# Two decoder layers on eight cores: opening in four steps, modulation scheduled apart from the norms, unpadded pool states

## Chip, cores and metric

The kernel runs on all 8 cores of one Trainium2 chip. Each core takes one prompt sequence (2048 tokens) and 16 of the 128 sample sequences (8 tokens each, 128 tokens together); nothing is exchanged between the cores. The metric is the device time of the slowest core in microseconds (us), lower is better.

## What is computed

Two layers over 1024 features. Every sublayer begins with an RMSNorm whose output is scaled and shifted by a modulation of the sequence's conditioning vector, and ends in a gated residual add. The part that the change touches, cut from the reference:

```
mod = silu(c) @ w_ada[l] + b_ada[l]                 # (B, 6D): 48 features of 128 a layer
sh1, sc1, g1, sh2, sc2, g2 = split(mod, 6)
h = rmsnorm(x, norm_mix[l]) * (1 + sc1) + sh1
# layer 0, mixer 0:
proj = h @ w_in0                                    # 1024 -> 2048
a, xin, bg, cg = split(proj, [512, 1024, 1536])
ya  = (trailing means of a over windows 2,4,8,16, minus a) @ w_pool, one 128x128 a group, * s_pool
yc  = depthwise causal conv (width 3) of cg * xin ;  yb = bg * yc
x   = x + g1 * (concat(ya, yb) @ w_out0)
# layer 1: a gating mixer of 128-position chunks instead
# every layer: x = x + g2 * (gelu(ga) * va) @ ffn_down, with ga, va = conv3(h @ ffn_up)
```

The sample sequences carry states in; that of the pooling is the last 15 rows of `a` of each sequence (`state_pool`).

## The kernel before, in words

Everything lies feature-major: 128 features on the partitions, tokens along the free dimension. A core's tokens are two streams: A is the first 1024 prompt tokens and the 128 sample tokens, B the other 1024 prompt tokens, with 8 features of x each in `xa`, `xs_t` and `xb` and the normalised input of a matmul in `ha` and `hb` (bf16). The stages follow in program order: mixer0(A), mixer0(B), ffn(A), ffn(B) and so on; while a stage runs on one stream, the next norm of the other stream is put between its pieces.

A Python program adds operations one after another to five engines' lists (`Sched`, L30): each list runs in that order, waits are derived from what an operation reads and writes. So the code's order is the order on each engine, and an operation that waits holds everything behind it on its engine. Three things set it around the change:

- Weights. Seven slots `wsl0` to `wsl6` hold a 1024x256 piece each (1 MB read as f32, 0.5 MB written as bf16 by a DMA of the POOL queue). `W.tick` (L340) issues the next piece of the list of uses for every slot that has come free; the pieces come in the order in which the program asks for them (`W.get`, L322). One bf16 piece of `w_ada` makes two features of the modulation: `g_ada` (L633) does 16 matmuls 128x17 into the bank `pN` and has DVE add the bias into `mod`; for scale features a second DVE operation follows.
- The background. `bg_stage` (L433) gives a stage a list of generators, and `pump` (L451), which is called between the pieces of a stage, advances them so that they are through after 17 of 20 parts of the calls. Before, norm and modulation are one list, woven one to one by `g_weave` (L583). A norm (`g_norm`, L574) squares the stream on ACT into `hb` or `ha` (scaled by 1/32), sums over the features with matmuls against ones into `pN` (`sums`), takes the power -0.5 on POOL, spreads the result over the partitions by matmuls (`bcast`), and applies it on DVE (`bg` from x, scale and rstd) and ACT (shift into `hb`).
- The opening (`program`, L1299), written by hand: x of A in two halves of 512 tokens (`load_x`), the squares, sums and scaling of each half (`scale_x` writes x times rstd into `xb`, which is free until B is loaded), the first eight modulation pieces between them (0 to 3 give the shifts, 4 to 7 the scales), and then `affine`, 16 operations on ACT and DVE by turns that make `ha`.

mixer0 (L743) runs four pool features P (input features 0 to 3) and four conv units C, of which each takes three features x, c and b. `P_open` (L758) does P0 and P1 of A together, 32 matmuls, k outermost. For the samples a pool feature needs its own extended row, 16 sequences times (15 old + 8 new) in a part of `R` (`ext_of`). Before, the host pads the states to that shape and four DMAs load them there; ACT then writes the 8 new columns of each sequence over the padding, and so waits for the load. `P_S2` (L795) is the pooling on DVE: up to four shifted additions of 1024 columns, the same for the samples, the subtraction. `P_S2b` (L833) is the 128x128 matmul of a group, `C_S1` (L859) a conv unit, `C_end` (L903) its product with b.

```
            act(E[2][:, 0:1024], PP[prx][:, :], AF.Copy, PK(prx), EK(2, 0, 1))
            if i >= 1:
                C_end(i - 1)
            else:
                P_S2(3)
            C_pre(i)
```

Of the kernel before, what the change touches and what calls it, by code (L numbers as in the profile page):

```python
# [152 lines left out]
def build_program():  # L153
# [12 lines left out]
    stp_d = din("stp", [128, 4, 16, 23])  # L166
# [264 lines left out]
    BG = {"early": [], "gens": [], "armed": True, "calls": {}, "subs": {}, "stage": None, "c": 0, "done": 0}  # L431

    def bg_stage(name, early, gens, armed):  # L433
        assert not BG["gens"] and not BG["early"]
        BG.update(stage=name, early=list(early), gens=list(gens), armed=False, c=0, done=0)
        if armed:
            bg_arm()

    def bg_sub():
        while BG["early"] or (BG["armed"] and BG["gens"]):  # L440
            q = BG["early"] or BG["gens"]
            try:
                next(q[0])
                if BG["armed"]:
                    BG["done"] += 1
                return True
            except StopIteration:
                q.pop(0)
        return False

    def pump():  # L451
        W.tick()
        if not BG["armed"]:
            bg_sub()
            return
# [12 lines left out]
    def bg_end():  # L468
# [3 lines left out]
        BG["calls"][BG["stage"]], BG["subs"][BG["stage"]] = BG["c"], BG["done"]  # L472
# [78 lines left out]
    def g_stats(st):  # L551
        nt = 3 if st.samp else 2
        for ti in range(2):
            for k0 in (0, 4):
                sq_main(st, ti, range(k0, k0 + 4))
                yield
# [3 lines left out]
        yield  # L560
        for ti in range(nt):
            sums(st, ti)
# [5 lines left out]
        yield  # L568
        bcast(st)
        yield  # L570
        rcopy(st)
        yield

# [8 lines left out]

    def g_weave(main, side, r):  # L583
        ms, ss, c = list(main), list(side), 0
        while ms or ss:
            q = ss if ss and (not ms or c % (r + 1) == r) else ms
            c += 1
            try:
                next(q[0])
                yield  # L590
            except StopIteration:
                q.pop(0)
# [40 lines left out]
    def g_ada(l, s):  # L633
# [16 lines left out]
        yield  # L650
# [91 lines left out]

    def mixer0(st):  # L743
# [13 lines left out]

        def P_open():  # L758
            sl = slots["a"] = W.get(("in0", 0))
            prs = [newpair(), newpair()]  # L760
            for ti in range(2):
                for k in range(8):
                    for g in range(2):
# [763 lines left out]
```

How the kernel before makes its waits and increments, by code:

```python
            def body(e, ops=ops, eng=eng):  # L134
                for op in ops:
                    for y in op.need:
                        if y.dma:
                            e.wait_ge(lane_sems[(y.eng, y.lane)], 16 * (y.gen + 1))
                        else:
                            e.wait_ge(sems[y.eng], y.val)
                    ins = op.fn(e)
                    if op.dma:
                        ins.then_inc(lane_sems[(eng, op.lane)], 16)
                    elif op.sig:
                        ins.then_inc(sems[eng], 1)
```

## Time and profile before

| what | value |
|---|---|
| median of 3 runs | 1557.12 us (1555.64 to 1557.77) |
| profiled execution, its own time | 1556.27 us |
| span of the profiled core (7, the slowest) | 1554.6 us |
| spans of the 8 cores | 1548.3 to 1554.6 us |
| PE / DVE / ACT / POOL busy | 92% / 67% / 51% / 21% of the span |
| chain of waits, share by engine | PE 79%, DVE 6%, ACT 6%, issue 4%, DMA 4% |
| mean granted TensorE clock | 0.979 |

The profile is that of the slowest core: of 1554.6 us its TensorE (PE) is busy for 1436.9. The other figures are read in that light: where PE is busy all the time, another engine's work costs nothing, and the 118 us in which it is not are what a new order of the work can win. The page's slices show where they lie: in forty slices PE is at 9 tenths or more from the fifth to the thirty-ninth, and at 1, 6, 5 and 8 tenths in the first four.

### The profile page before, as it was taken

The page shows a single profiled execution, that of the slowest core. Times are in us where ns is not written, and L with a number is a line of the kernel's source. Part 1 is how long each engine was busy: PE and PEld are TensorE (multiplying, and loading weights), DVE is VectorE, ACT ScalarE, POOL GpSimd, SP SyncE. Part 2 cuts the span into 40 slices and gives each one's busy share as a digit, 9 for nine tenths or more (in the row PEclk, how much of TensorE's full clock was granted, in tenths as well). Part 3 has the DMA queues.
Part 4 walks back from the last instruction along what each step waited for, and adds up shares of the span by engine and source line. Part 5 has one row for each costly group of instructions (what it writes and reads, how often), then busy time and mean ns, then how long its engine had stood idle before and what let it go on. Part 6 is the DMA issues. An engine that isn't in the chain of part 4 may idle for free.

```text
span 1554.6 us, 26494 instructions; the slowest of 8 cores (1548.3 to 1554.6 us)
## 1 busy us (share of the span) xinstructions
PE 1436.9 (92%) x9294; PEld 752.6 (48%) x9294; DVE 1037.4 (67%) x1071; ACT 793.2 (51%) x966; POOL 326.6 (21%) x769
## 2 busy tenths in 40 slices
PE   1658999999999999999999999999999999999996
PEld 1334544445545544444456566544554444444444
DVE  1656557568687777759754533656768977677886
ACT  2235145457475555737555425445746654664552
POOL 2112112112232122223212101112212222222210
PEclk9979999999999999999999999999999999999998
DMA  9957656654568645445643821644444454446523
GB/s 209 201 133 126 96 83 102 114 95 77 105 111 132 121 69 94 83 82 90 118 71 63 150 42 28 101 79 83 88 80 80 74 87 68 81 76 138 124 45 109
DMA packets 62678, 151.93 MB, mean 98 GB/s; under 512 B 13010, under 2 KB 28498, under 8 KB 62036
## 3 DMA queue, kind: packets, MB, share of 16 engines
q0 software_dynamic: 33984, 120.34, 48.4%
q1 hardware_dynamic: 28564, 29.90, 6.2%
q8 instruction: 76, 1.25, 0.3%
q14 instruction: 54, 0.44, 0.1%
HBM read 252.68 MB, written 17.85 MB: 174 GB/s over the span
## 4 chain that ended last, share of the span: by engine, by line
PE 79%; DVE 6%; ACT 6%; issue 4%; DMA 4%; POOL 1%; DVEq 0%; ACTq 0%; POOLq 0%; SPq 0%
PE pp L382 72%; PE pS L382 5%; PE pN L382 2%; DMA wsl<-w_ada 2%; DMA xb<-xp 1%; ACT hb L401 1%; ACT E L401 1%; ACT Y L401 1%; DVE Y L404 1%; ACT ha L401 1%; DVE Y L408 1%; DVE ha L404 1%; DVE bg L404 1%; DVE xb L408 1%; DVE xb L404 1%
## 5 line engine op out<-in xcount | busy, mean ns | idle before, releaser
L404 DVE SCALAR_TENSOR_TENSOR Y<-E,par_t,Y 128x1184 f32<-128x1184 f32 (+1 forms) x368 | 502.2, 1367 | 246.1 <-ACT Y L401 232.3
L382 PE MATMUL pp<-ha,wsl 128*128 128x512 bf16 (+1 forms) x1840 | 427.6, 384 | 6.8 <-DVE ha L1328 3.8
L382 PE MATMUL pp<-R,wsl 128*128 128x512 bf16 (+2 forms) x1928 | 421.8, 375 | 0.8 <-DVE xb L404 0.4
L382 PE MATMUL pp<-hb,wsl 128*128 128x512 bf16 x1792 | 399.9, 382 | 3.7 <-DVE xb L404 2.9
L401 ACT ACTIVATE E<-pp 128x1024 f32<-128x1024 f32 x192 | 196.1, 1022 | 329.6 <-PE pp L382 325.4
L382 PEld LDWEIGHTS pp<-R,wsl 128*128 128x128 bf16 x1928 | 185.2, 98 | 212.0 <-issue 1.7
L382 PEld LDWEIGHTS pp<-hb,wsl 128*128 128x128 bf16 x1792 | 174.9, 98 | 214.0 <-issue 11.5
L401 ACT ACTIVATE Y<-E,par_t 128x1184 f32<-128x1184 f32 (+1 forms) x184 | 240.6, 1307 | 67.0 <-DVE R L408 17.2
L382 PEld LDWEIGHTS pp<-ha,wsl 128*128 128x128 bf16 x1840 | 176.9, 99 | 201.1 <-issue 21.1
L411 POOL COPY cffn<-E 128x2 f32<-128x2 f32 x176 | 78.2, 444 | 442.5 <-ACT E L401 442.5
L408 DVE TENSOR_TENSOR R<-Y 128x1184 bf16<-128x1184 f32 (+1 forms) x86 | 112.2, 1305 | 5.8 <-ACT Y L401 5.4
L401 ACT ACTIVATE Y<-Y 128x1184 f32<-128x1184 f32 (+1 forms) x88 | 97.7, 1110 | 17.3 <-DVE Y L404 17.2
L404 DVE SCALAR_TENSOR_TENSOR xa<-pp,mod,xa 128x1024 f32<-128x1024 f32 x64 | 79.9, 1279 | 33.8 <-PE pp L382 33.8
L404 DVE SCALAR_TENSOR_TENSOR xb<-pp,mod,xb 128x1024 f32<-128x1024 f32 (+3 forms) x80 | 83.5, 1066 | 27.1 <-PE pp L382 27.1
L401 ACT ACTIVATE Y<-pp 128x1024 f32<-128x1024 f32 x33 | 33.5, 1016 | 114.8 <-PE pp L382 78.3
L370 POOL DMA_DIRECT2D wsl<-ffn_up x88 | 46.8, 532 | 189.1 <-PE pS L382 86.6
L382 PE MATMUL pN<-sc_t,wsl 128*128 128x17 bf16 x768 | 26.8, 172 | 61.3 <-DMA wsl<-w_ada 31.4
L382 PE MATMUL pS<-ha,wsl 128*128 128x128 bf16 x896 | 69.2, 221 | 10.5 <-ACT E L401 6.2
L382 PEld LDWEIGHTS pS<-ha,wsl 128*128 128x128 bf16 x896 | 57.7, 99 | 35.0 <-issue 18.9
L401 ACT ACTIVATE E<-pS 128x128 f32<-128x128 f32 x92 | 24.4, 265 | 89.0 <-PE pS L382 82.9
L401 ACT ACTIVATE hb<-xb 128x512 bf16<-128x512 f32 (+2 forms) x88 | 46.0, 580 | 35.2 <-DVE xb L404 23.9
L382 PEld LDWEIGHTS pN<-sc_t,wsl 128*128 128x128 bf16 x768 | 25.4, 98 | 73.3 <-issue 66.9
(110 smaller groups left out, 1011.6 us busy)
## 6 DMA issues: line engine op xcount, KB each, us to landing
wsl<-ffn_up POOLq DMA_DIRECT2D x88, 512.0 KB, 5.6
wsl<-w_ada POOLq DMA_DIRECT2D x48, 512.0 KB, 8.2
wsl<-ffn_down POOLq DMA_DIRECT2D x32, 448.0 KB, 4.9
wsl<-w_in POOLq DMA_DIRECT2D x16, 512.0 KB, 8.0
wsl<-w_out POOLq DMA_DIRECT2D x16, 512.0 KB, 6.9
wsl<-ffn_down POOLq DMA_DIRECT2D x16, 512.0 KB, 5.4
wsl<-w_uv POOLq DMA_DIRECT2D x16, 512.0 KB, 6.9
o_ffn_s<-E SPq DMA_DIRECT2D x88, 80.0 KB, 4.9
```

The lines of the kernel that those rows point to most:

```text
L370: add("pool", lambda e, s=s, src=src, n=n: e.dma_start(out=wsl[s][:, 0:n], in_=src), writes=[("w", s)], dma=True)
L382: add("pe", lambda e, l=l, r=r, i=i: e.matmul(out_ap, lhsT=l, rhs=r, start=(start and i == 0), stop=(stop and i == n - 1)), reads=rk, writ ...
L401: add("act", lambda e: e.activation(out=out, in_=in_, func=func, **kw), reads=reads, writes=writes)
L404: add("dve", lambda e: e.scalar_tensor_tensor(out=out, in0=in0, scalar=scalar, in1=in1, op0=op0, op1=op1), reads=reads, writes=writes)
L408: add(eng, lambda e: e.tensor_tensor(out=out, in0=in0, in1=in1, op=op), reads=reads, writes=writes)
L411: add("pool", lambda e: e.tensor_copy(out=out, in_=in_), reads=reads, writes=writes)
```

## The change

Six edits:

1. Opening. The DVE share of the second half's squares goes to ACT; modulation pieces 2 and 3 come later; pieces 4 to 7 are each followed by the affine operations of two features (both halves), and the 32 matmuls of P0 and P1 are done in four groups of eight (`open_k`), each one step behind its affine operations. The weights of P0 and P1 are asked for before modulation piece 4.
2. `W.tick()` stands in `setup` behind the loads of x instead of ahead of it.
3. The background has two lists. Norms are advanced as before; modulation is a `side` list of its own, at most two half pieces a call, spread over 97% of a stage's calls (from a quarter on in mixer0(A)), and no new piece starts between a norm's sums and its rstd copy (`lock`). A norm squares two features a step instead of four. In mixer0(A) the norm of B starts after 16 idle steps (before, 10).
4. In C unit 0 the pooling of group 3 (`P_S2(3)`) moves from behind the x matmuls to behind the c product on DVE, and the first conv operation on ACT to behind the b copy.
5. The pool states come unpadded (128x960) in one DMA to a place of their own; POOL copies them into the extended rows, four copies of 16x15.
6. ACT's writing of the new sample columns no longer waits for the load.

```
@@ pump
-        n, c = BG["subs"][BG["stage"]], BG["calls"][BG["stage"]]
+        (n, m), c = BG["subs"][BG["stage"]], BG["calls"][BG["stage"]]
         target = -(-n * BG["c"] * 20 // max(1, 17 * c))
         while BG["done"] < target:
             if not bg_sub():
                 break
+        f = (BG["c"] / c - BG["s0"]) / (0.97 - BG["s0"])
+        for _ in range(2 if BG["sdone"] + 3 < m * f else 1):
+            if BG["sdone"] < m * f and not (BG["lock"] and BG["sdone"] % 2 == 0):
+                bg_sub("side", "sdone")
@@ g_stats
-            for k0 in (0, 4):
-                sq_main(st, ti, range(k0, k0 + 4))
+            for k0 in range(0, 8, 2):
+                sq_main(st, ti, range(k0, k0 + 2))
                 yield
...
+        BG["lock"] = True
         for ti in range(nt):
             sums(st, ti)
...
+        BG["lock"] = False
@@ mixer0
+        def ext_hist(g):
+            sa, sk = rsp_f32(5120, 960)
+            pcopy(ap3(exts[g][0], 23)[:, :, 0:15], ap3(sa[:, g * 240:(g + 1) * 240], 15), sk, [("exh", g)])
...
                 act(ap3(a, 23)[:, :, 15:23], v3(so[g][0]), AF.Copy, so[g][1], k)
+                ext_hist(g)
@@ C_S1
             if i >= 1:
                 C_end(i - 1)
-            else:
-                P_S2(3)
...
+            if i == 0:
+                P_S2(3)
+            else:
+                yinit()
@@ program
-        adas(0, 2)
+        adas(0, 1)
         sums(A_, 0)
         rstd_pow(0, 4)
-        adas(2, 3)
+        adas(1, 2)
         bcast_part(0)
         scale_x(0)
-        for k in range(8):
-            if k % 2 == 0:
-                sq_main(A_, 1, (k,))
-            else:
-                stt(A_.h[:, k, 512:1024], xseg(A_, k, 512, 512), 1.0 / 1024, xseg(A_, k, 512, 512), ALU.mult, ALU.mult,
-                    xK(A_, k, 1), hK(A_, k, 1))
-        adas(3, 5)
+        sq_main(A_, 1, range(8))
         sums(A_, 2)
         sums(A_, 1)
         rstd_pow(4, 5)
-        adas(5, 6)
+        adas(2, 3)
         bcast_part(1)
         bcast_part(2)
-        adas(6, 7)
+        scale_x(1)
...
-        scale_x(1)
-        adas(7, 8)
-        for ti in range(2):
-            for k in range(8):
-                affine(ti, k, "act" if k % 2 == 0 else "dve")
+        adas(3, 4)
+        open_get()
+        for q in range(4):
+            adas(4 + q, 5 + q)
+            for ti in range(2):
+                for k in (2 * q, 2 * q + 1):
+                    affine(ti, k, "act" if k % 2 == 0 else "dve")
+            if q >= 1:
+                open_k(A_, (2 * q - 2, 2 * q - 1))
...
-        bg_stage("m0A", [], [g_idle(10), g_weave(norm_gens(B_, 0), ada_gens(0, 8, 18), 1)], True)
+        open_k(A_, (6, 7))
+        bg_stage("m0A", [g_idle(16)] + norm_gens(B_, 0), ada_gens(0, 8, 18), True, 0.25)
```

The order on the engines shows three places. First PE in the opening: `sc_t` rows are modulation pieces, `ones_bf` rows the sums, `ident` rows the broadcasts, `pp<-ha` the matmuls of P0 and P1.

```order
-L382 MATMUL pN<-sc_t,wsl 128x17 x32
-L382 MATMUL pp<-ha,wsl 128x512 x32
+L382 MATMUL pN<-sc_t,wsl 128x17 x48
+L382 MATMUL pp<-ha,wsl 128x512 x8
+L382 MATMUL pN<-sc_t,wsl 128x17 x16
+L382 MATMUL pp<-ha,wsl 128x512 x8
+L382 MATMUL pN<-sc_t,wsl 128x17 x16
+L382 MATMUL pp<-ha,wsl 128x512 x16
```

The last two modulation pieces now stand between the groups of the opening's matmuls.

Second, ACT in mixer0(A), behind the copy of P2 out of PSUM (`E<-pp`); `hb<-xb` are the squares of B, `R<-pN,par_t` and `R<-pp,par_t` the copies of a finished pool group, `E<-pS` and `E<-pp` those of a feature. Before:

```order
L401 ACTIVATE E<-pp 128x1024
L401 ACTIVATE hb<-xb 128x512 x4
L401 ACTIVATE R<-pN,par_t 128x16x8
L401 ACTIVATE R<-pp,par_t 128x1024
L401 ACTIVATE hb<-xb 128x512 x4
L401 ACTIVATE R<-pS 128x16x8
L401 ACTIVATE hb<-xb 128x512 x4
L401 ACTIVATE E<-pp 128x1024
```

The same place in the changed kernel:

```order
L401 ACTIVATE E<-pp 128x1024
L401 ACTIVATE R<-pN,par_t 128x16x8
L401 ACTIVATE R<-pp,par_t 128x1024
L401 ACTIVATE R<-pS 128x16x8
L401 ACTIVATE E<-pp 128x1024
L401 ACTIVATE R<-pN,par_t 128x16x8
L401 ACTIVATE R<-pp,par_t 128x1024
L401 ACTIVATE E<-pS 128x128
L401 ACTIVATE hb<-xb 128x512 x2
```

The first squares of B stood ahead of the copies of groups 0 and 1 and of P3; now they stand behind them and behind the sample copy of C unit 0's x.

Third, PE around C unit 0 of the changed kernel, from the matmul of pool group 1 (`Y2`, `wsl3`) on; with slot numbers, which tell the weights apart: `wsl6` holds x, `wsl0` c, `wsl1` b, `wsl5`, `wsl4` and `wsl2` modulation.

```order
L382 MATMUL pp0<-Y2,wsl3 128x512 x2
L382 MATMUL pS<-ha,wsl6 128x128 x8
L382 MATMUL pp1<-ha,wsl6 128x512 x16
L382 MATMUL pN<-sc_t,wsl4 128x17 x16
L382 MATMUL pS<-ha,wsl0 128x128 x8
L382 MATMUL pp2<-ha,wsl0 128x512 x16
L382 MATMUL pS<-ha,wsl1 128x128 x8
```

And POOL, which issues the loads of these slots:

```order
L370 DMA wsl5<-w_ada 128x2048
L370 DMA wsl6<-w_in0 128x2048
L370 DMA wsl0<-w_in0 128x2048
L370 DMA wsl1<-w_in0 128x2048
L411 COPY R<-R 128x16x15 x2
L370 DMA wsl4<-w_ada 128x2048
```

The modulation piece in `wsl4` is used between x and c; its load stands behind those of x, c and b and behind two of the new copies, which wait for the states.

## Rows read from the trace of the kernel before

**Rows 1.** Busy time by stretch (us, then busy us and count by engine, clock, DMA)

```profile
0.00:56.60 56.60, 13.14 (x220) 10.98 (x221) 16.40 (x37) 13.00 (x22) 12.30 (x43) 1.00 0.98 194
56.60:156.00 99.40, 73.23 (x587) 38.82 (x588) 58.27 (x92) 43.90 (x70) 14.98 (x34) 0.86 0.76 152
156.00:264.00 108.00, 101.37 (x670) 50.84 (x669) 65.53 (x76) 41.29 (x55) 19.34 (x36) 0.97 0.65 96
```

**Rows 2.** Waits, 66 to 110 us: in total, times, longest

```profile
PE pN L382 <- ACT R L401: 10.6, 1, 10.6
...
PE pN L382 <- DVE mod L408: 5.2, 1, 5.2
...
PE pS L382 <- ACT R L401: 3.4, 1, 3.4
```

**Rows 3.** Timeline, 0 to 70 us: start, busy, what, count

```profile
33.39 2.18 ACT L401 ACTIVATE ha<-xa 128x512 bf16<-128x512 f32 x4
...
42.19 1.41 PE L382 MATMUL pN<-ones_bf,ha 128*128 128x1 bf16 x40 [0.45 <-DVE mod L408]
...
47.99 0.27 ACT L401 ACTIVATE rstd<-pN 128x128 f32<-128x128 f32 x1
...
50.71 4.90 DVE L408 TENSOR_TENSOR xb<-xa,rstd 128x512 f32<-128x512 f32 x8
...
56.61 8.42 PE L382 MATMUL pp<-ha,wsl 128*128 128x512 bf16 x30 [3.77 <-DVE ha L1328]
```

**Rows 4.** DMA issues by window (at 2.9 and 22.9 us): KB, us to landing

```profile
xa<-xp SPq DMA_DIRECT2D x1, 2048.0 KB, 29.4
...
wsl<-w_in POOLq DMA_DIRECT2D x1, 512.0 KB, 28.7
```

**Rows 5.** Timeline, 66 to 170 us

```profile
82.10 2.19 ACT L401 ACTIVATE hb<-xb 128x512 bf16<-128x512 f32 x4 [5.89 <-DMA xb<-xp]
...
98.88 1.01 PE L382 MATMUL pS<-ha,wsl 128*128 128x128 bf16 x8
...
99.69 6.06 PE L382 MATMUL pp<-ha,wsl 128*128 128x512 bf16 x16
...
105.59 0.61 PE L382 MATMUL pS<-ha,wsl 128*128 128x128 bf16 x8
...
112.99 3.62 PE L382 MATMUL pp<-ha,wsl 128*128 128x512 bf16 x16
...
163.74 10.52 PE L382 MATMUL pp<-hb,wsl 128*128 128x512 bf16 x48
```

**Rows 6.** DMA issues by window (at 56.1, 58.4 and 76.0 us): KB, us to landing

```profile
R<-stp SPq DMA_DIRECT2D x1, 184.0 KB, 9.0
...
R<-stp SPq DMA_DIRECT2D x1, 184.0 KB, 13.5
...
wsl<-w_ada POOLq DMA_DIRECT2D x1, 512.0 KB, 15.8
```

**Rows 7.** DMA queues, 65 to 71.5 us, then 71.5 to 82 us: packets, MB, share

```profile
q1 hardware_dynamic: 587, 1.29, 62.0%
q0 software_dynamic: 104, 0.35, 35.7%
...
q1 hardware_dynamic: 162, 2.39, 65.8%
q0 software_dynamic: 150, 0.55, 33.8%
```

**Rows 8.** DVE alone, by stretch: the pooling of groups 1 and 3

```profile
69.60:75.20 5.60, 5.09 (x9) 0.70 0.95 285
99.30:108.45 9.15, 8.32 (x14) 0.71 0.01 2
```

**Rows 9.** POOL, groups by form: busy, mean ns of one

```profile
L411 POOL COPY E<-cpool 128x15 f32<-128x15 f32 x4 | 2.6, 657 | 0.2 <-POOL csc L411 0.2
```

**Rows 10.** Waits of PE, 156 to 264 us

```profile
PE pN L382 <- DVE mod L408: 2.4, 2, 2.1
```

**Rows 11.** Waits of PE, 264 to 500 us

```profile
PE pS L382 <- ACT E L401: 5.1, 4, 2.8
```

More of the change, by code:

```diff
@@ L429, in store, with bg_stage, bg_sub @@
         add("sp", lambda e: e.dma_start(out=out, in_=in_), reads=reads, writes=[("out", octr[0])], dma=True)
[L431 to L441, printed above, removed]
-            try:
-                next(q[0])
-                if BG["armed"]:
-                    BG["done"] += 1
+    BG = {"gens": [], "side": [], "armed": True, "calls": {}, "subs": {}, "stage": None, "c": 0, "done": 0,
+          "sdone": 0, "lock": False, "s0": 0.0}
+    def bg_stage(name, gens, side, armed, s0=0.0):
+        assert not BG["gens"] and not BG["side"]
+        BG.update(stage=name, gens=list(gens), side=list(side), armed=armed, c=0, done=0, sdone=0, s0=s0)
+    def bg_sub(which="gens", cnt="done"):
+        while BG[which]:
+            try:
+                next(BG[which][0])
+                BG[cnt] += 1
                 return True
             except StopIteration:
-                q.pop(0)
+                BG[which].pop(0)
         return False
@@ L471, in bg_end @@
             pass
-        BG["calls"][BG["stage"]], BG["subs"][BG["stage"]] = BG["c"], BG["done"]
+        while bg_sub("side", "sdone"):
+            pass
+        BG["calls"][BG["stage"]], BG["subs"][BG["stage"]] = BG["c"], (BG["done"], BG["sdone"])
     def run(gen):
@@ L568, in g_stats @@
         yield
+        yield
         bcast(st)
@@ L581, in norm_gens @@
         return [g_norm(st, which)]
[L583 to L592, printed above, removed]
     def g_idle(n):
@@ L741, in ext_of, with open_get, open_k @@
         return R_t[:, b // 2: b // 2 + 736].bitcast(F32), RK(b, 1472)
+    opn = {}
+    def open_get():
+        opn["sl"] = W.get(("in0", 0))
+        opn["prs"] = [newpair(), newpair()]
+    def open_k(st, ks):
+        sl, prs = opn["sl"], opn["prs"]
+        for ti in range(2):
+            for k in ks:
+                for g in range(2):
+                    gemm(PP[prs[g]][:, ti * 512:(ti + 1) * 512], PK(prs[g], ti),
+                         [(wap(sl, k, g), st.h[:, k, ti * 512:(ti + 1) * 512])], [("w", sl)], [hK(st, k, ti)],
+                         start=(k == 0), stop=(k == 7))
     def mixer0(st):
@@ L812, in P_S2 @@
                 e3 = ap3(a, 23)
+                k = list(k) + [("exh", g)]
                 c3, lns, ck = e3, 23, k
@@ L885, in C_S1, with yinit @@
             tt(E[ei][:, 2:1026], PP[prc][:, :], E[2][:, 0:1024], ALU.mult, PK(prc) + EK(2, 0, 1), EK(ei, 1))
-            act(Y[ei][:, 0:n], E[ei][:, 2:2 + n], AF.Identity, EK(ei) + ["par"], YK(ei), scale=par(wb + 2),
-                bias=par(P_SCB + i))
+            def yinit():
+                act(Y[ei][:, 0:n], E[ei][:, 2:2 + n], AF.Identity, EK(ei) + ["par"], YK(ei), scale=par(wb + 2),
+                    bias=par(P_SCB + i))
+            if i == 0:
+                P_S2(3)
+            else:
+                yinit()
             pump()
@@ L1286, in setup @@
         load_x(A_, 1)
+        W.tick()
         for g in range(2):
@@ L1376, in program @@
            bgk01 + [("mod", k) for k in range(8)], [("h", 0, k, 2) for k in range(8)])
-        for g in range(4):
-            a, k = ext_of(g)
-            load(a.rearrange("p (b w) -> p b w", w=23), stp_d[:, g, :, :], k, [("mod", 15)])
+        sa, sk = rsp_f32(5120, 960)
+        load(sa, stp_d[:, :], sk, [("mod", 15)])
         load(hist_t[:, :, :, :], sts_d[:, :, :].rearrange("p (r c) w -> p r c w", c=2), [("hist", 0), ("hist", 1)],
```

37 lines of the change are left out of this document (16 added, 21 removed).

## Prediction

> **What bounds the kernel now.** I first read the busy time by stretch, to see where PE is not busy, then the waits of those stretches, then the timeline around each wait for what held the engine that was waited for. Over the whole kernel PE is busy for all but 118 us of its span. Of these, 43.5 us lie ahead of 56.6 us (busy 13.1), 26.2 us in mixer0(A), from 56.6 to 156 us (busy 73.2 of 99.4), and 6.6 us in mixer0(B) [rows 1]. The other 1290 us hold 41 us. So the change can win something in the first two stretches, and little elsewhere.
>
> In mixer0(A) three waits make 19.2 of the 26.2 us: 10.6 for ACT's copies of a pool group, 5.2 for DVE's bias add and 3.4 for ACT's copies of sample columns [rows 2]. The first two have one cause. ACT is in order, and its squares of B stand ahead of the copies (second order excerpt); the squares waited for the load of `xb`, which came at 82.1 us [rows 5]. DVE's add of a modulation piece stands behind ACT's copy through the bank `pN`. So PE stood still until B had landed, twice, once for each half. When it went on, it was slow: 16 matmuls of 512 columns took 6.06 us, against 3.62 for the same 16 at 113 us [rows 5], which is 2.4 us more. The granted clock in the stretch of pool group 3's pooling, which covers them, is 0.71 [rows 8]; half is the lower of the two levels, 1.2 GHz against 2.4.
>
> **Opening.** Each edit on the chain that leads to the 32 matmuls of P0 and P1:
> - The second half of x lands at 2.9 + 29.4 = 32.4 us [rows 4]. Four squares take 2.18 us on ACT [rows 3], so eight take 4.4 and the sums can begin at 36.9 us. Before they began at 42.2, since DVE's share of the squares waited for its scaling of the first half. From the sums' start to the last rstd copy's end 6.1 us pass (42.2 to 48.3), here to 43.0; the half that the scaling needs is copied 0.5 us sooner, 42.5.
> - Scaling takes DVE 4.9 us [rows 3], to 47.4 (before 55.6). From there to the first of the 30 matmuls 1.0 us passed. Now there also lie the sample's scaling, 1.2 (one of the eight scalings takes 0.61, this has twice the columns), and one more modulation piece, about 1.0 (both estimates): first matmul at 50.6.
> - The last modulation piece is bound by its weights. Nine 1 MB pieces come through the POOL queue whatever their order; the ninth, before that of P0 and P1, landed at 22.9 + 28.7 = 51.6 us [rows 4]. Now the ninth is modulation piece 7, and 51.6 stays. It is needed behind two groups of matmuls, after 54 us, so it is not late.
> - The matmuls took 8.4 us [rows 3]. With two pieces between them (0.6 each) and half a microsecond for the alternation with the affine operations, 10.1: the end comes at 61 us, against 65.0. **Minus 4.** Ends: nothing slow and no gap gives 5.5; all 32 at 0.38 us (6.06 / 16 [rows 5]) is 12.1 + 1.2 and gives 1.
>
> `W.tick` behind the loads changes nothing that the chip sees: x goes through SP's list, weights through POOL's, and the first seven loads stay first in POOL's. I cost it at zero; no cover is needed, since it adds no instruction.
>
> **Mixer0(A) up to C unit 0.** The load of the states is issued after the last scale feature, near 58 us. Four padded loads landed 9.0 us (first) to 13.5 us (last) after their issue [rows 6]; the one load with longer rows is nearest to the first: 67 us. ACT no longer waits for it (3.4 us less for PE [rows 2], of which 1.5 stay for ACT's two copies of P0 and P1 at 1.0 each). But POOL copies now wait, and DVE's sample pooling behind them. The nearest row for a copy of 240 columns is POOL's 128x15 copy at 0.66 us [rows 9]; a copy of sixteen times the columns may take no longer, or, at three times that, 2 us. With 0.7 the first is done at 67.7. DVE then has the rest of group 0, 2.3 us (an estimate: one 1024-column operation of 1.2 and small ones), and 5.6 of group 1 [rows 8], done at 75.6. PE needs this for the group 1 matmul that stands ahead of C unit 0 (third excerpt), so x of unit 0 starts at 76 us. Before it started at 98.9 [rows 5]: 23 us ahead. B's squares wait now where nothing of groups 0, 1 and P3 stands behind them.
>
> **The wait that takes its place.** Behind x stands a modulation piece with `wsl4`. Its load is issued only when P0 and P1 have released the slot and POOL has done two copies, at 68 us, and it is fourth in POOL's queue, behind x, c and b. From 61 us SP's two 2 MB loads of `xb` compete. A weight load issued at 76 us amid them took 15.8 us [rows 6]; that would be 84. From 71.5 to 82 us the queues moved 162 and 150 packets, one to one, though SP's carried four times the bytes [rows 7], so a weight piece (about 140 packets) passes for each half of `xb`. Half 1 of `xb` began at 71.5 and took 10.5 us, to 82.1; now they begin near 66, with b beside the first and this piece beside the second: 66 + 2 x 10 = 86. I take 86, near the 84. x is done at 80, so PE stands for 6 us and runs slow behind it, 2.8 us with the sample matmuls.
>
> The Trainium skill (DMA: Bandwidth & Descriptors, Queues, rings and completion order) says that each DMA engine takes its queues by turns, a packet at a time. By it the piece lands with the second half of `xb`, as above, 86. The trace has a stretch that speaks against it: from 65 to 71.5 us SP's queue moved 587 packets to POOL's 104 [rows 7]. At that ratio the piece would land behind both halves, after 91, and the total below would be 5 us higher.
>
> **From c of unit 0 to mixer0(B).** Before, 105.6 to 163.7 us, 58.1 us [rows 5]. Of these 26.2 - 19.2 = 7.0 are PE waits, which I remove; added are the 64 sum matmuls of B, which stood ahead (40 took 1.41 [rows 3], so 2.3), and the slow stretch of 2.8. New waits: DVE now does the c product first and group 3's pooling (9.15 us [rows 8]) behind it, then the taps (3 us) and the unit's product (1.5). With c at 94 us that ends near 109, and c of unit 1 is done near 108; bounded by nothing below and by one pooling, 9 us, above, I take 1.5. 58.1 - 7.0 + 2.3 + 2.8 + 1.5 = 57.7, from 86.5 to 144.2. Before 163.7: **minus 19.5**, the opening's 4 included. The eight later modulation pieces of this stage are the same in number. Their loads find SP's queue empty (the first three are issued near 111, needed from 118), so I cost them at nothing; were `xb` still in flight, one would cost its 15.8 - 7 us.
>
> **Mixer0(B) and later.** In mixer0(B) the sums waited 2.1 us for a modulation add [rows 10] that stood behind group 3's pooling on DVE, and the clock fell: another 2.4 as above. With the pooling behind the c product the add is not held. I take **minus 4**, between 0 (another wait comes) and 6.6, all the idle time there [rows 1]. In ffn(A) PE waits 5.1 us for ACT's copies [rows 11] while four squares at a time stand ahead; two at a time should shorten it: **minus 1**, between 0 and 5.1. The 30 modulation pieces of the later stages are only spaced otherwise.
>
> **Sum.** 19.5 + 4 + 1 = 24.5. The profiled execution took 1556.3 us as a whole (its span is 1554.6), the median of the runs is 0.8 above it: 1556.3 - 24.5 + 0.8 = 1532.6, say **1532 us**.
>
> **Rivals.**
> - *The piece in `wsl4` is in time* (1524 us). If its load gets through beside `xb` as fast as 15.8 us less the queue ahead, near 80, the 6 us wait and the 2.8 of slow clock go: 8.8 less. For it: the row's queue was as full. Against: the packets one to one. Chance 0.17.
> - *The mixer stays late* (1542). The ratio 587 to 104 puts c of unit 0 at 91.5 (5 more), and DVE, which has its pooling behind the c product, passes on some 5 us to unit 1. Chance 0.25.
> - *The four steps don't do what they say* (1536). DVE's and ACT's affine operations and PE wait for each other by turns at the lower clock, and the opening ends where it did, 65: the 4 us are missing. For it: the first matmuls come after 50 us of little work. Chance 0.10.
> - *Slower than before* (1563). The later 30 modulation pieces are no longer woven into the norm's steps. In mixer0(B) one such piece held PE for 2.1 us and cost 2.4 more in clock, 4.5. If that befell the pieces of ffn(A), ffn(B) and mixer1(A), the 24.5 us are gone from the sixth one on; with seven more than the one removed the time is 1532 + 7 x 4.5 = 1563. Against: in the stretch from 264 to 500 us, which holds most of the twelve pieces of ffn(A), no wait for a modulation add is among PE's waits, and ACT's copies are all that it waits for [rows 11]. Chance 0.04.
>
> **Numbers.** The forecast has 0.44, the rivals 0.17, 0.25, 0.10 and 0.04. Its own ends: the opening 1 to 5.5, mixer0(B) 0 to 6.6, ffn(A) 0 to 5.1, the new DVE wait 0 to 9. The range takes in the early piece with a little of ffn(A)'s wait (1524 - 3) and the late mixer with no gain in mixer0(B) and a shorter one in the opening (1542 + 6): 1521 to 1548. A measurement of this kernel can tell 0.2%, 3 us, from no change. All cases but the last are faster by more; 0.02 is kept for a mixture that ends between: faster 0.94, same 0.02, slower 0.04.
>
> **What the changed profile would show.** ACT's wait for `xb` no longer ahead of PE waits; the first matmul of P0 near 51 us, the last near 61; x of unit 0 near 76; PE waiting for `w_ada` near 80 to 86 (none: the first rival); the first matmul on `hb` near 144. I am wrong if that one comes after 155, if the load of the states lands after 72 us, or if PE's idle time behind 264 us has grown by more than 5.

## The result, and the profile after

The change makes the kernel faster: 1542.87 us, the median of 4 runs (1542.21 to 1543.79), against 1557.12 before in the same comparison; the ratio is 0.9906, 95% interval 0.9893 to 0.9919. That is some 14 us less where 25 were forecast, inside the range of 1521 to 1548 and 11 us above the forecast's own 1532. Runs in which the cores of a die were slowed by a disturbance are left out of every time and ratio, here and below.

The page of the changed kernel: its span, busy times, and of the slices PE and PE's clock.

```profile
span 1540.4 us, 26482 instructions; the slowest of 8 cores (1534.2 to 1540.4 us)
...
PE 1431.2 (93%) x9294; PEld 748.5 (49%) x9294; DVE 1035.8 (67%) x1067; ACT 796.6 (52%) x970; POOL 325.3 (21%) x773
...
PE   2668978999999999999999999999999999999996
...
PEclk9989989999999999999999999999999999999998
```

The profiled execution took 1542.21 us. Two things are to be seen: PE's idle time went from 118 us to 109 only, and the first seven slices, the opening and both streams' first mixer, still hold most of it (78 us up to 264 us). Busy time by stretch (us, then busy us and count of PE, PEld, DVE, ACT and POOL, clock, DMA share, GB/s), the stretches of [rows 1] first:

```profile
0.00:56.60 56.60, 18.22 (x235) 13.29 (x236) 16.07 (x35) 16.77 (x28) 11.73 (x42) 1.00 0.99 196
56.60:156.00 99.40, 75.26 (x626) 41.09 (x624) 60.51 (x93) 46.37 (x72) 19.60 (x42) 0.91 0.80 156
156.00:264.00 108.00, 92.05 (x608) 45.55 (x607) 62.26 (x72) 37.26 (x51) 17.68 (x34) 0.93 0.57 88
```

and the last part of the program, from the first matmul of ffn(A) on, in the changed kernel:

```profile
271.80:1540.00 1268.20, 1237.92 (x7799) 645.26 (x7797) 894.46 (x866) 692.76 (x817) 276.25 (x656) 0.99 0.51 91
```

and before:

```profile
268.70:1554.00 1285.30, 1244.45 (x7799) 649.81 (x7797) 894.70 (x866) 692.28 (x817) 279.97 (x656) 0.99 0.51 90
```

With PE's own landmarks as the borders, the 14.2 us of span come about like this, with the wrong sign in the middle row:

| stretch | before | after | difference | forecast |
|---|---|---|---|---|
| start to the first matmul on `hb` | 163.7 | 155.1 | -8.7 | -19.5 |
| mixer0(B), to the first matmul of ffn(A) | 105.0 | 116.7 | +11.7 | -4 |
| ffn(A) to the end | 1285.9 | 1268.6 | -17.3 | -1 |

These are marks of one core, the slowest. Among the eight cores of one execution they differ by 3 to 4 us (the first matmul on `hb` comes at 159.7 to 163.7 before and at 152.9 to 156.2 after), so 2 or 3 us in one cell say little. The medians of the eight cores tell the same here: -8.4, +11.7 and -18.4.

PE's waits from 56 to 156 us: in total, times, longest.

```profile
PE pN L382 <- DVE mod L408: 15.8, 3, 10.7
PE pN L382 <- DVE Y L408: 4.9, 1, 4.9
PE pN L382 <- DMA wsl<-w_ada: 1.9, 1, 1.9
```

The 10.6 us for ACT behind the squares of B [rows 2] are gone. A wait of the same length stands in their place: 10.7 us for DVE's add of a modulation piece. And from 156 to 264 us:

```profile
PE pN L382 <- DVE mod L408: 11.8, 3, 6.5
PE pp L382 <- POOL rs L408: 2.2, 1, 2.2
```

where before DVE's adds made 2.4 us, 2.1 the longest [rows 10]. Both long ones have one picture. DVE's timeline from 90 to 106 us (start, busy, what, count, idle before it and releaser):

```profile
90.91 1.23 DVE L408 TENSOR_TENSOR E<-pp,E 128x1024 f32<-128x1024 f32 x1 [4.33 <-PE pp L382]
92.05 1.23 DVE L408 TENSOR_TENSOR Y<-E 128x1038 f32<-128x1038 f32 x1
93.38 3.90 DVE L408 TENSOR_TENSOR Y<-Y 128x1036 f32<-128x1036 f32 x3
97.20 2.05 DVE L408 TENSOR_TENSOR R<-R 128x352 f32<-128x352 f32 x4
...
102.45 3.02 DVE L404 SCALAR_TENSOR_TENSOR Y<-E,par_t,Y 128x1184 f32<-128x1184 f32 x2 [1.30 <-ACT Y L401]
105.39 0.19 DVE L408 TENSOR_TENSOR mod<-pN,par_t 128x34 f32<-128x34 f32 x1
```

and PE's at its end:

```profile
84.59 0.55 PE L382 MATMUL pN<-sc_t,wsl 128*128 128x17 bf16 x16 [2.04 <-DVE mod L408]
85.00 0.94 PE L382 MATMUL pS<-ha,wsl 128*128 128x128 bf16 x8
...
105.72 0.27 PE L382 MATMUL pN<-Y,wsl 128*128 128x128 bf16 x1 [10.68 <-DVE mod L408]
```

The c product (90.91) is followed by the pooling of group 3 (92.05 to 101.1) and the taps (102.45 to 105.4); the add of the modulation piece that PE has put into `pN` stands behind all of them, and the pool matmul of group 2 needs the same bank. In mixer0(B) it is the sums that need it: 6.48 us at 218.58, with the pooling from 211.76 to 218.3 on DVE.

### The profile page after: what moved, and what is told of

It is laid out like the page before. It is cut to its first block, busy times and chain, and to the rows that moved or that the text cites. A ratio compares the mean times of both kernels' runs of the same rounds, so it can differ in the third digit from the quotient of the medians.

```text
span 1540.4 us, 26482 instructions; the slowest of 8 cores (1534.2 to 1540.4 us)
## 1 busy us (share of the span) xinstructions
PE 1431.2 (93%) x9294; PEld 748.5 (49%) x9294; DVE 1035.8 (67%) x1067; ACT 796.6 (52%) x970; POOL 325.3 (21%) x773
## 4 chain that ended last, share of the span: by engine, by line
PE 80%; DVE 7%; ACT 5%; issue 4%; DMA 3%; POOL 0%; DVEq 0%; SPq 0%; ACTq 0%; POOLq 0%
PE pp L382 73%; PE pS L382 5%; DVE Y L404 2%; DMA xa<-xp 2%; PE pN L382 2%; ACT ha L401 2%; ACT Y L401 2%; ACT E L401 1%; DVE Y L408 1%; DVE R L408 1%; DVE bg L404 1%; DMA R<-stp 1%; ACT hb L401 1%; DVE ha L404 1%; DVE xb L404 1%
## 5 line engine op out<-in xcount | busy, mean ns | idle before, releaser
L382 PEld LDWEIGHTS pS<-ha,wsl 128*128 128x128 bf16 x896 | 57.8, 99 | 30.7 <-issue 15.1
L401 ACT ACTIVATE ha<-xa 128x512 bf16<-128x512 f32 x80 | 43.3, 615 | 17.5 <-DMA xa<-xp 17.5
## 6 DMA issues: line engine op xcount, KB each, us to landing
wsl<-w_in POOLq DMA_DIRECT2D x16, 512.0 KB, 10.1
```

Of the source, the lines that this page charges most:

```text
L382: add("pe", lambda e, l=l, r=r, i=i: e.matmul(out_ap, lhsT=l, rhs=r, start=(start and i == 0), stop=(stop and i == n - 1)), reads=rk, writ ...
L401: add("act", lambda e: e.activation(out=out, in_=in_, func=func, **kw), reads=reads, writes=writes)
```

## Experiments

Each kernel is given by what it changes; `...` marks what is cut from a diff. `hb` is the time of the first matmul on `hb`, then the length of mixer0(B) and of all behind it, from the profile of its slowest core; the last column has the medians of the same three over the eight cores of that execution. The ratio is to the kernel before on the same chip.

| kernel | ratio, 95% interval | hb | mixer0(B) | behind it | medians of 8 cores |
|---|---|---|---|---|---|
| before | 1 | 163.7 | 105.0 | 1285.9 | 162.5, 103.0, 1286.3 |
| changed | 0.9906 (0.9893 to 0.9919) | 155.1 | 116.7 | 1268.6 | 154.1, 114.7, 1267.9 |
| hold | 0.9950 (0.9930 to 0.9969) | 157.2 | 116.8 | 1269.3 | 154.8, 116.2, 1267.8 |
| p3_back | 0.9815 (0.9793 to 0.9838) | 146.5 | 108.0 | 1270.8 | 147.0, 103.8, 1269.7 |
| p3_A | 0.9883 (0.9867 to 0.9899) | 148.6 | 115.0 | 1270.7 | 147.5, 112.3, 1266.8 |
| ps2_only | 0.9883 (0.9868 to 0.9899) | 156.2 | 107.8 | 1270.7 | 154.9, 107.8, 1267.8 |
| e4_only | 1.0054 (1.0036 to 1.0072) | 165.4 | 107.7 | 1288.6 | 164.1, 106.8, 1286.2 |
| no_side | 1.0032 (1.0020 to 1.0045) | 164.7 | 107.4 | 1286.3 | 163.6, 106.0, 1285.1 |
| open_only | 1.0031 (1.0003 to 1.0059) | 168.7 | 111.5 | 1291.7 | 163.8, 107.0, 1292.0 |
| pb_sq4 | 0.9916 (0.9886 to 0.9946) | 157.3 | 104.9 | 1275.2 | 154.9, 105.5, 1273.9 |
| pb_noopen | 0.9862 (0.9842 to 0.9882) | 154.5 | 106.7 | 1271.3 | 151.7, 107.0, 1268.1 |
| pb_padded | 0.9831 (0.9803 to 0.9860) | 149.5 | 109.1 | 1266.8 | 149.7, 105.2, 1267.3 |
| pb_early | 0.9800 (0.9772 to 0.9829) | 144.4 | 108.0 | 1271.0 | 144.7, 104.2, 1267.9 |
| pe_s35 | 0.9857 (0.9836 to 0.9878) | 150.9 | 112.7 | 1267.6 | 149.2, 110.2, 1267.7 |

The profile of open_only is not to be compared stretch by stretch: that execution took 1573.6 us where the median of its runs is 1558.1, and on its slowest core the granted clock was 0.81 from 160 to 230 us although PE was busy all the time.

### Edit 4: the place of the pooling

**p3_back**, the changed kernel with edit 4 undone:

```diff
             if i >= 1:
                 C_end(i - 1)
+            else:
+                P_S2(3)
             C_pre(i)
...
-            if i == 0:
-                P_S2(3)
-            else:
-                yinit()
+            yinit()
             pump()
...
-            if i == 0:
-                yinit()
             for tap in (1, 0):
```

> The changed kernel with its fourth edit undone: the pooling of group 3 behind the x matmuls of unit 0 again, for both streams. Theory: PE's waits of 10.7 us (mixer0(A)) and 6.5 us (mixer0(B)) for a modulation add come from the add standing behind that pooling on DVE while the bank pN is held; with the pooling a product earlier the one in A is at most 3 us, the c product comes 3 us later, and the slow clock behind it goes: 1532 to 1537 us. Rival: DVE is simply short of time there, the wait moves to the c product and to the matmuls behind it: 1542 us, the same.

It took 1526.8 us, a ratio of 0.9815 against 0.9906: edit 4 cost about 15 us (15.1 in the spans). That is 5 us less time than the theory had, and its rival (1542) is out. Both stretches answer, -8.6 up to `hb` and -8.7 in mixer0(B); by the medians -7.1 and -10.9. PE's waits from 56 to 264 us are now many and short, none over 4.1 us:

```profile
PE pN L382 <- DVE mod L408: 13.2, 7, 2.9
PE pN L382 <- DVE Y L408: 4.1, 1, 4.1
PE pS L382 <- DVE mod L408: 3.2, 1, 3.2
```

**hold** asks whether it is the held bank alone: no new modulation piece starts between the issue of the pooling and the pool matmul of group 2 of the changed kernel.

```diff
             if i == 0:
+                BG["hold"] = True
                 P_S2(3)
...
                 P_S2b(n - 2)
+                if n == 4:
+                    BG["hold"] = False
...
-            if BG["sdone"] < m * f and not (BG["lock"] and BG["sdone"] % 2 == 0):
+            if BG["sdone"] < m * f and not ((BG["lock"] or BG["hold"]) and BG["sdone"] % 2 == 0):
```

> The changed kernel, but no new modulation piece begins between the issue of group 3's pooling and the pool matmul of group 2, in both streams; the pooling stays where the change put it. Theory: no matmul result lies in pN while DVE pools, so PE's waits of 10.7 and 6.5 us for the add go, with the 2 to 4 us of slow clock behind each; what stays is DVE's own lateness with unit 1's product, about 5 us: 1526 to 1533 us. Rival: the wait is DVE's load and not the held bank; the same wait stands at the next thing that PE needs from DVE: 1540 us or more.

The pool matmul ran at 92.97 without a wait, and the kernel was still no faster than the changed one: 1548.0, a ratio of 0.9950 against 0.9906. The next rows of PE, and ACT's behind them, show the wait again, on another engine:

```profile
92.97 0.22 PE L382 MATMUL pN<-Y,wsl 128*128 128x128 bf16 x1
93.03 0.59 PE L382 MATMUL pp<-Y,wsl 128*128 128x512 bf16 x2
103.31 0.58 PE L382 MATMUL pN<-sc_t,wsl 128*128 128x17 bf16 x16 [9.69 <-ACT R L401]
```

```profile
99.47 1.37 ACT L401 ACTIVATE Y<-E,par_t 128x1184 f32<-128x1184 f32 x1 [5.15 <-DVE fix L408]
100.75 2.17 ACT L401 ACTIVATE hb<-xb 128x512 bf16<-128x512 f32 x4
102.82 0.35 ACT L401 ACTIVATE R<-pN,par_t 128x128 bf16<-128x128 f32 x1
```

ACT's first conv operation writes a buffer `Y` that the pooling of group 3 still reads, so it waits for the pooling's last operation; squares and the copy out of `pN` stand behind it. The pooling behind the c product thus holds two engines, DVE by its length and ACT through `Y`. In mixer0(B) the hold came too late to keep a piece out, and the sums waited 6.48 us as before. The theory of the bank alone fell; its rival held by the time (1540 us or more), though the next wait was for ACT, which stood behind DVE through `Y`, and not for DVE itself.

**p3_A** undoes edit 4 in stream A alone, **ps2_only** undoes half of it in both streams.

```diff
             if i >= 1:
                 C_end(i - 1)
+            elif st is A_:
+                P_S2(3)
...
-            if i == 0:
+            if i == 0 and st is not A_:
                 P_S2(3)
             else:
                 yinit()
...
-            if i == 0:
+            if i == 0 and st is not A_:
                 yinit()
```

> The changed kernel (1542.87 us) with edit 4 undone in mixer0 of stream A alone. Undone in both streams it took 16 us off (1526.83), of which 8.6 us were there at the first matmul of hb. Theory: the pooling behind the c product costs in each stream by itself, 8 to 9 us in A and the rest in B: 1533 to 1536 us, and the sums of mixer0(B) still wait over 5 us for DVE. Rival: B only inherits what A lost (an earlier A leaves its norm and its loads in time): 1526 to 1529 us.

```diff
             if i >= 1:
                 C_end(i - 1)
+            else:
+                P_S2(3)
...
-            if i == 0:
-                P_S2(3)
-            else:
+            if i != 0:
                 yinit()
```

> The changed kernel (1542.87 us) with only the first half of edit 4 undone: the pooling of group 3 stands behind the x matmuls again, the first conv operation on ACT stays behind the b copy. Theory: the place of the pooling carries the whole cost (it holds DVE's adds of modulation, and ACT through the buffer Y1): 1526 to 1529 us. Rival: the late first conv operation keeps DVE's taps, which stand ahead of the next adds, waiting for ACT by 1 to 2 us a stream and more: 1531 to 1537 us.

Both took 0.9883, some 6 us less than the changed kernel by the spans (1534.2 and 1534.7 against 1540.4), in different places. p3_A has the gain up to `hb` (148.6) and keeps the wait of 6.48 us at the sums: each stream pays by itself, A 6.5 us (155.1 to 148.6; by the medians 6.6) and B 7.0 (115.0 against p3_back's 108.0; by the medians 8.5). Its time, 1536.5, is at the upper end of its theory (1533 to 1536), and the rival that B only inherits is out. ps2_only has nothing up to `hb` (156.2) and its gain in mixer0(B) (107.8, by the medians 6.9 of the 10.9 us that p3_back gains there). So in A the place of the pooling alone is not the matter. DVE of ps2_only after its c product:

```profile
93.13 1.21 DVE L408 TENSOR_TENSOR E<-pp,E 128x1024 f32<-128x1024 f32 x1
101.75 3.02 DVE L404 SCALAR_TENSOR_TENSOR Y<-E,par_t,Y 128x1184 f32<-128x1184 f32 x2 [7.41 <-ACT Y L401]
104.69 0.19 DVE L408 TENSOR_TENSOR mod<-pN,par_t 128x34 f32<-128x34 f32 x1
```

DVE has nothing to do for 7.4 us, because ACT's first conv operation now stands behind the copy of b, which waits for b's matmuls, and the add that PE waits for stands behind the taps. The second half of edit 4 alone (the late conv operation) thus makes the add come at 104.7, as late as both halves together (105.4); the first half alone was not run. In B the add that the sums need is ahead of the taps, and the pooling's place decides most there: the sums start at 213.1 after a wait of 0.2 us. The forecast of 1526 to 1529 for ps2_only failed and its rival (1531 to 1537) held.

**e4_only** is edit 4 alone on the kernel before.

> The kernel before (1556 to 1557 us) with edit 4 alone. Theory: the pooling behind the c product costs by itself, in whatever schedule, since the pool matmul of group 2 shares the bank pN with a modulation piece whose add stands behind it: 1561 to 1572 us, with a wait of PE for DVE of over 5 us between 105 and 125 us. Rival: here the squares of B hold ACT longer and modulation pieces stand elsewhere, so DVE has room for the pooling, and edit 4 is harmful only together with the modulation list: 1554 to 1558 us.

1563.2, slower than before by 8 us, as its theory had it: it costs in the old schedule too. The pool matmul of group 2 waited 4.98 us for the add, and in the kernel before there was no such wait. By the medians 1.6 us of the cost lie up to `hb` and 3.8 in mixer0(B). It is about half of that in the new schedule; a likely reason, not tested, is that PE stood 11.0 us for ACT ahead of it (to 92.9), behind the load of `xb`, which left DVE time.

### The opening

**open_only** is the kernel before with edit 1 (and edit 2, the place of `W.tick`), **pb_noopen** is p3_back with the old opening.

```diff
-        adas(0, 2)
+        adas(0, 1)
...
+        open_get()
+        for q in range(4):
+            adas(4 + q, 5 + q)
...
```

> The kernel before with the opening in four steps and nothing else of the change. Theory: the opening's own gain is real, the last of the 32 first matmuls ends at 60 to 61 us instead of 65, but ACT still waits for the load of B behind it, so PE stands until B has landed as before, and of the 5 us only those 1 to 2 are kept by which B's load is issued earlier: 1555 to 1556 us. Rival: the 5 us pass to the end: 1552 us.

```diff
-        open_get()
-        for q in range(4):
-            adas(4 + q, 5 + q)
...
+        adas(6, 7)
...
+        scale_x(1)
+        adas(7, 8)
...
+        open_get()
+        open_k(A_, range(8))
```

> Base: the changed kernel with edit 4 undone (1526.83 us). Here the opening is that of the kernel before (edit 1 undone). Theory of the prediction (the four steps are worth 4 us, and every us reaches the end because ACT no longer waits for B): the last of the 32 matmuls at 65 us instead of 60.1, and 1530 to 1532 us. Rival: the states, which land at 68.3 us whatever the opening does, take the gain on DVE: 1526 to 1528 us with PE's wait for Y below 1 us.

Alone the four steps bring nothing: 1.0031, the median run 1558.1 us, slower than its theory (1555 to 1556) and far from its rival (1552). Its profile shows PE waiting 6.2 and 9.1 us for ACT's copies between 56 and 100 us; ACT stands in front of the first for the padded states and in front of the second for `xb`. Where ACT waits for neither any more the steps are worth 7.3 us by the spans, 0.9862 against 0.9815; that is more than the 4 us of the theory (1530 to 1532 us against 1534 measured). The opening's own gain is there in both, by its last matmul: 65.0 to 61.4 us in open_only (59.7 on its fastest core), 65.4 to 59.5 from pb_noopen to p3_back. It reaches the end only once nothing behind it waits for a load that comes when it comes. The rival of pb_noopen, that the states' landing takes the gain, did not hold.

### The modulation list and the squares

**no_side** is the changed kernel with edit 3 undone (woven list, ten idle steps, squares by four, and also three idle steps fewer inside a norm and one more in a modulation piece, which belong to the edit), **pb_sq4** is p3_back with squares by four alone.

```diff
-        bg_stage("m0A", [g_idle(16)] + norm_gens(B_, 0), ada_gens(0, 8, 18), True, 0.25)
+        bg_stage("m0A", [g_idle(10), g_weave(norm_gens(B_, 0), ada_gens(0, 8, 18), 1)], [], True)
...
```

> The changed kernel with its third edit undone: norm and modulation woven into one list again, ten idle steps, squares by four. Theory: the squares of B stand ahead of the copies of groups 0 and 1 again, the waits for B of 16 us return, and the later stages (ffn(A), mixer1) lose the some 14 us that they gained: 1557 to 1562 us. Rival: the later gain is not from the third edit; then about 1550 us.

```diff
-            for k0 in range(0, 8, 2):
-                sq_main(st, ti, range(k0, k0 + 2))
+            for k0 in (0, 4):
+                sq_main(st, ti, range(k0, k0 + 4))
```

> Base: the changed kernel with edit 4 undone (1526.83 us). Here a norm squares four features a step instead of two; the side list and its lock stay. Theory: the squares in pairs are what took away PE's waits for ACT in ffn(A), mixer1 and ffn(B) (5.1 us for E from 264 to 500 us, 3.7 for rstd, 3.4 and 4.1 in mixer1 before), so these come back, and 1532 to 1538 us. Rival: the modulation's own list is what took them away (the norm comes through at an even pace), and the size of the steps is worth nothing: 1526 to 1529 us.

Without edit 3 the kernel is slower than the one before (1560.1, as its theory had it), PE waits 10.2 us for ACT behind the load of B again, and the part behind ffn(A) is back at 1286.3 us: all of the 17 us won there are edit 3's. PE's longest wait from 500 to 787 us in no_side is that of before,

```profile
PE pN L382 <- ACT rstd L401: 3.7, 1, 3.7
```

and in the changed kernel none there is longer than 1.8.

pb_sq4 took 1540.9 us, above its theory (1532 to 1538) and its rival (1526 to 1529). Behind ffn(A) it is 4.4 us longer than p3_back (1275.2 against 1270.8), but most of the waits that its theory expected back do not come back: in ffn(A) PE waits 0.7 us for ACT and not the 5.1 of [rows 11], and the 3.7 for `rstd` is absent. What comes is a new single wait of 8.4 us in mixer1(A), where the sums of a norm need the bank of a modulation add:

```profile
827.77 2.96 PE L382 MATMUL pN<-ones_bf,hb 128*128 128x1 bf16 x64 [8.39 <-DVE mod L408]
```

So the late gain does not rest on the squares' size in ffn(A) and ffn(B); at most 4 of the 17 us are the squares' and some 13 the rest of edit 3. Which of the rest does it (the list of its own, its pace, the lock, the idle steps) was not taken apart. In mixer0(A) `hb` comes at 157.3 instead of 146.5 (medians 154.9 and 147.0). PE waits there for an add behind group 3's pooling (4.9), twice for a pooling itself (4.2 together), and 5.2 us for an add that stands behind the taps and the norm's scaling `bg`: no single cause, and which of the shifted pieces costs what stays open.

### The states and the piece in `wsl4`

**pb_padded** is p3_back with the padded states in four loads, **pb_early** is p3_back with the states' load behind modulation feature 5, **pe_s35** is pb_early with the modulation list from 0.35 of the calls on.

```diff
-        sa, sk = rsp_f32(5120, 960)
-        load(sa, stp_d[:, :], sk, [("mod", 15)])
+        for g in range(4):
+            a, k = ext_of(g)
+            load(a.rearrange("p (b w) -> p b w", w=23), stp_d[:, g, :, :], k, [("mod", 15)])
...
```

> Base: the changed kernel with edit 4 undone (1526.83 us). Here the states come padded as in the kernel before, in four loads, so that ACT's writing of the sample columns waits for them and POOL copies nothing (edits 5 and 6 undone). Theory: ACT stands behind the later of the four loads (13.5 us to landing before), the copies of P2 and the pool groups behind it come 2 to 4 us later: 1529 to 1531 us. Rival: DVE needs the states at the same time anyway, and nothing moves: 1526 to 1528 us.

```diff
         adas(3, 4)
+        sa, sk = rsp_f32(5120, 960)
+        load(sa, stp_d[:, :], sk, [("mod", 5)])
         open_get()
...
-        sa, sk = rsp_f32(5120, 960)
-        load(sa, stp_d[:, :], sk, [("mod", 15)])
```

> Base: the changed kernel with edit 4 undone (1526.83 us). Here the load of the pool states is issued behind modulation feature 5 instead of 15, some 10 us earlier. Theory: their landing at 68.3 us sets the start of group 0's pooling on DVE, so PE's wait for Y (4.1 us, 56 to 100 us) goes or falls below 1.5 and x of C unit 0 comes 3 to 5 us earlier: 1521 to 1524 us. Rival: the load shares the queues with the last weights of the opening, whose landing moves by 1 to 2 us, and P0 starts later than 50.5 us by as much; or DVE's own work is the limit: 1526 to 1529 us.

```diff
-        bg_stage("m0A", [g_idle(16)] + norm_gens(B_, 0), ada_gens(0, 8, 18), True, 0.25)
+        bg_stage("m0A", [g_idle(16)] + norm_gens(B_, 0), ada_gens(0, 8, 18), True, 0.35)
```

> The kernel with edit 4 undone and the states' load issued 10 us earlier (1524.1 us, PE standing 7.5 us for the modulation weights in wsl4 between x and c of unit 0), with the modulation list starting at 0.35 of the calls of mixer0(A) instead of 0.25: x, c and b of unit 0 are loaded ahead of the modulation piece, which is used in the middle of c. Theory: the transfer that lands last is in time there, 4 to 8 us go: 1516 to 1520 us. Rival: the queue is full until B has landed, so whatever piece is fourth lands at 84 us, and b or the next modulation piece is waited for instead: 1522 to 1526 us.

pb_padded: 0.9831, from two runs, not to be told from p3_back (0.9793 to 0.9838), so neither its theory nor its rival is settled, although ACT waits there three times for a load (3.90, 2.85 and 4.51 us) and PE 7.5 us for ACT. Edits 5 and 6 move a wait from ACT to DVE and are worth at most a few us.

pb_early: the states are issued at 38.1 us. PE's wait for `Y` went, as forecast, and x of unit 0 begins 5.3 us earlier than in p3_back, at 71.8. c of unit 0 does not:

```profile
71.83 0.61 PE L382 MATMUL pS<-ha,wsl 128*128 128x128 bf16 x8
72.49 3.40 PE L382 MATMUL pp<-ha,wsl 128*128 128x512 bf16 x15
83.41 0.58 PE L382 MATMUL pN<-sc_t,wsl 128*128 128x17 bf16 x16 [7.52 <-DMA wsl<-w_ada]
83.83 1.01 PE L382 MATMUL pS<-ha,wsl 128*128 128x128 bf16 x8
```

The load of this piece was issued at 62.50 and took 20.7 us, to 83.2; in the changed kernel it was issued at 69.07 and took 15.0, to 84.1. Issued 6.6 us sooner it landed 0.9 sooner. With the order changed so that x, c and b come first (pe_s35), c begins at 79.3, but b waits until 88.3 for DVE, which pools group 3, and a modulation piece in mixer0(B) waits 9.3 us for its weights; 0.9857 (1532.6 us, two runs), slower than pb_early. Theory (1516 to 1520) and rival (1522 to 1526) both missed, the rival by less. pb_early, at 1524.1 us and 0.9800, is the fastest of all these kernels and beats the changed one by 1%; the step from p3_back to it is within the intervals.

## Why the prediction was right in its sign and wrong in its size

The forecast said faster by 25 us, and the kernel is faster by 14. It went right up to c of unit 0 and wrong behind it, and the total would be further off but for a gain that it had put at nothing.

- **Opening: right.** First matmul at 50.47 (50.6 forecast), the last of 32 done at 60.15 (61).

```profile
50.47 3.57 PE L382 MATMUL pp<-ha,wsl 128*128 128x512 bf16 x8 [0.69 <-ACT ha L401]
...
56.46 3.69 PE L382 MATMUL pp<-ha,wsl 128*128 128x512 bf16 x16
```

- **Up to C unit 0: right within 2.5 us.** The states were issued at 57.3 and landed 11.0 us later (67 forecast, 68.3 measured), POOL's two copies took 0.72 us together against 0.7 for one. From POOL's row on everything is 1.3 late and DVE's chain another 1.2: x of unit 0 at 78.50 instead of 76.

```profile
68.40 0.72 POOL L411 COPY R<-R 128x240 f32<-128x240 f32 x2 [10.72 <-DMA R<-stp]
...
78.50 0.61 PE L382 MATMUL pS<-ha,wsl 128*128 128x128 bf16 x8
```

- **"The wait that takes its place": the time right, the wait shorter.** The piece landed at 84.1 (86 forecast), and c of unit 0 began at 85.00 (86.5). But x was done only at 82.6 (80 forecast), so PE stood 2.0 us and not 6. The profile puts this to an add behind group 2's pooling, which ended at 84.4; without it the load would have held PE until 84.1, nearly as long. That B's loads set the landing is what pb_early shows. The rival with 587 packets to 104 would have c at 91.5, and is out; so is the one with the piece in time.
- **"From c of unit 0 to mixer0(B)": here it failed.** 57.7 us were forecast, 70.1 came (85.0 to 155.1). PE is idle for 15.7 of them (10.7, 3.1 and 1.9) where the forecast had 1.5, and its busy part, 54.4, is 1.8 below the 56.2 of the sum. Two terms are wrong. "I take 1.5" for the pooling behind the c product, between nothing and 9: it compares the pooling's end with c of unit 1 as a chain of products, and doesn't follow the add that stands behind the pooling in DVE's list, nor ACT behind its conv operation. The wait was 10.7 us, above the bound; what it cost was inside it, since edit 4 undone in A gives back 6.5 (p3_A) to 8.6 (p3_back). And "7.0 are PE waits, which I remove" gives no reason why none should come in their place. With edit 4 undone PE still waits 8.3 us behind c, all for adds of modulation pieces: 3.2 behind group 3's pooling, 1.5 behind the taps, 0.8 and 2.7 behind the norm's scaling `bg`, where the list of its own now puts them. The last of them in p3_back:

```profile
134.48 0.55 PE L382 MATMUL pN<-sc_t,wsl 128*128 128x17 bf16 x16 [2.74 <-DVE mod L408]
...
130.17 4.06 DVE L404 SCALAR_TENSOR_TENSOR bg<-xb,mod,rstd 128x512 f32<-128x512 f32 x6
134.15 0.18 DVE L408 TENSOR_TENSOR mod<-pN,par_t 128x34 f32<-128x34 f32 x1
```

- **"Mixer0(B)": the wrong sign.** "With the pooling behind the c product the add is not held" holds only for an add that is issued ahead of the c product. A piece came between: the add stands behind product and pooling, and the sums behind the add. Forecast -4, measured +11.7. With edit 4 undone in both streams the stage is at 103.8 us by the medians, against 103.0 before and 114.7 after, so nearly all of it is edit 4's: 8.5 by its place in B alone (p3_A against p3_back), and the rest only with it in A too. The slowest core of p3_back has 108.0 and is an exception: the other seven have 103.6 to 104.4. The gain of 4 that was forecast did not come in p3_back either.
- **"30 modulation pieces only spaced otherwise": mis-sized.** -1 forecast for ffn(A) and nothing for the rest, -17.3 measured for all that lies behind, of which ffn(A)'s waits for ACT are 4.0 (5.1 to 1.1). The prediction looks for waits up to 500 us and takes the 41 us of idle time behind 264 us as thin everywhere. Part of them were single waits, in ffn(B) and mixer1, for a norm's results (`rstd` 3.7, `rs` 2.5 and 2.3) and its squares, which edit 3 removes or shortens: idle 40.9 to 30.3, and the same 7799 matmuls are busy 6.5 us less.
- **The sum** was near by luck, through two errors that oppose each other: -17.3 for -1, and +3 for -23.5. Of the rivals the late mixer (1542) gives the time to the microsecond, with part of its mechanism: DVE did pass its pooling on, as a wait of 10.7 us in A and not 5, but the other half of its price, the landing behind both halves of B, did not come, and nothing in it foresaw mixer0(B) or the later gain. The case slower than before, pieces unwoven from the norm that hold PE in ffn(A), ffn(B) and mixer1, is the reverse of what happened there. Of the three signs of being wrong one came, by a hair: the first matmul on `hb` at 155.07, after 155.

## What to carry to other kernels

When an operation is moved on an in-order engine, list what is now behind it, small operations above all: 0.2 us adds that free a bank were worth 10 us of PE. Follow the buffers too, since a moved pass holds a second engine through what it still reads. A wait taken away shows up in the row behind it until the long pass itself is elsewhere (hold), and a gain ahead of a fixed landing is worth little until that landing is no longer waited for (the opening in open_only, x of unit 0 in pb_early). Idle time far from the edited lines deserves a list of its single waits before it is costed at zero. And where several cores run the same program, compare a stage by their median: the slowest core alone hid here that mixer0(B) is back where it was once edit 4 is undone.

## What the runs showed of the hardware

- The weight load of 512 KB in `wsl4`, which shares the DMA engines with two of 2 MB, did not land a fixed time after its issue: it took 20.7 us from 62.5 (pb_early), 20.0 from 63.3 (pe_s35) and 15.0 from 69.1 (changed), and landed at 83 to 84 us each time. From 71.5 to 82 us of the changed kernel the DMA share is 1.02 at 288 GB/s, and from 74 to 82 us the two queues move 120 and 114 packets, one to one as before; from 84 us on SP's queue takes little (22% from 84 to 86 us, against 62% from 82 to 84).
- After its long stand PE is slow again. From 99 to 106 us, while it waits, the granted clock is 0.50, the lower level of 1.2 GHz; the eight matmuls at 107.50 take 2.63 us, where eight take 1.89 at 110.38. DVE alone in that stretch:

```profile
99.00:106.00 7.00, 5.31 (x9) 0.50 0.11 20
```

- One load of 480 KB for the states took 11.0 us (10.1 in p3_back, 9.5 in pb_noopen). Four of 184 KB took 9.0 to 13.5 before. They differ in bytes, in rows and in the moment of issue, and no run here takes these apart.
